# A mixture-of-experts layer at the end of a three-layer program: the order in which the first two pairs of heads choose their experts and fetch the expert rows

## The chip, the cores and the metric

The program runs on one core of one Trainium2 chip. Its time is the device time of one execution in microseconds (us); several executions are timed and their median is given. Everything is computed in float32; weights are split into a high and a low part so that three fast matrix products make one of nearly full precision.

## What is computed

Two blocks of one kind and one of another run after each other on 256 tokens of width 2048. The change touches only the last sublayer, which looks up single-neuron experts ("PEER") for each token:

```python
q = (hb @ w_query).reshape(PEER_BLOCK, PEER_HEADS, 2, D_KEY // 2)
s = jnp.einsum('thpc,hpnc->thpn', q, sub_keys)
top_s, top_i = lax.top_k(s, PEER_TOPK)                      # 16 of 128, twice per head
cand_s = (top_s[:, :, 0, :, None] + top_s[:, :, 1, None, :]).reshape(PEER_BLOCK, PEER_HEADS, -1)
best_s, best_j = lax.top_k(cand_s, PEER_TOPK)               # 16 of 256 per head
idx = jnp.take_along_axis(cand_i, best_j, axis=-1)          # expert numbers
g = jax.nn.softmax(best_s, axis=-1)
a = jax.nn.gelu(jnp.einsum('thkd,td->thk', jnp.take(u, idx, axis=0), hb), approximate=False)
out = jnp.einsum('thk,thkd->td', g * a, jnp.take(v, idx, axis=0))
```

There are 8 heads, 16 experts per head and token, and two blocks of 128 tokens. Each expert is one row of 2048 numbers (8 KB) in the table u and one in the table v, both of 16384 rows in HBM.

## The kernel before

One function, `order()`, yields the whole program as a list of steps, and each engine's function walks that same list and issues its own part of each step. So the order of the yields is the order of every engine's queue. Long pieces of work are generators in a "lane" (X, Y, M); `pump` advances a lane by so many steps, `drain` runs it to its end.

The work of the last sublayer, for which `order()` has the lines below "late_loads":

- **The query projection**, 32 weight pieces (numbered q = 0 to 31 here, four column groups of 8). SyncE loads each piece of 512 KB into one of the 4 slots of `ring`; ScalarE rounds it to the high part `wH` (L603); VectorE subtracts to get the low part `wL` (L1102, "the split"), which also frees the ring slot; TensorE multiplies (24 matmuls of 128x256 a piece, out to `tp`). There are 3 buffers of wH and wL, and the split for piece q + 2 stands ahead of piece q.
- **The choice of experts** (`choose(i)`) for a pair of heads and a block of 128 tokens; there are 8 such pairs, i = 0 to 7. It runs on VectorE: the scores of four lists are reduced to their best 16 (`top16`: max, index, replace, max, index), sums of pairs are formed, the best 16 of 256 taken for each of two heads, and the expert numbers are worked out by comparison with a row of constants (L1628 to L1641) and written to `ix` (L1646). Then come the transposed numbers `ixT` and the softmax weights. In all 10 steps of the lane X.
- **The dot products** (`dot(i, j)`, j = 0 to 31): GpSimd issues an indirect DMA (L2303) that gathers, for column j, one row of u for each of the 128 tokens into a slot (128x2048, 1 MB), and VectorE multiplies it with the tokens and sums (L1729).
- **The v blocks** (`vmix(i, b)`, b = 0 to 7): 4 gathers each from v into slots, and 32 small matmuls (L1770, `pp<-slot,S`) that add weighted rows to the result in `pp`. They need `gelu(i)` on ScalarE and `blend(i)` on VectorE (L1739 to L1746), which need all 32 dots of the pair.

There are 11 slots (`gs`): three in P and SY and two in x (0 to 4), two that lie over the weight ring (5, 6; free once the last split is done) and four in `late` (7 to 10; they lie over the projection's operands and are free once its last matmul is done). `slots()` gives the gathers, in the order of issue, their slots: the first 16 go round slots 0 to 4, after that all 11 go round. A gather into a slot waits until the dot or v block that used it is done.

In the kernel before, choose(0) is advanced 1.25 steps a piece in the pieces 8 to 15, and then drained; dot (0, j) goes with piece 16 + j. The other 16 dots of pair 0 follow the projection, with choose(1) advanced 0.65 steps a dot between them. From pair 1 on, each pair's 32 dots have the 8 v blocks of the pair before among them (one block behind every fourth dot), and choose(i + 1) at 0.42 steps a dot.

## Time and profile before

| | us |
|---|---|
| median of 3 runs | 3189.14 |
| lowest and highest | 3184.85, 3191.65 |
| the profiled execution | 3189.19 |
| its span, first to last instruction | 3187.3 |
| VectorE busy | 1688.7 |
| TensorE busy | 2167.2 |
| GpSimd busy | 790.4 |

The profile counts microseconds from the start of the span. PE is TensorE (PEld its weight loads), DVE VectorE, ACT ScalarE, POOL GpSimd. The last sublayer runs from about 1800 us to the end. In a timeline row the first number is the start, the second the duration, and the brackets at its end hold the idle time before it and what ended it. "DMA share" is the mean busy share of the 16 DMA engines and "GB/s" what they moved. The granted clock of TensorE is 1.00 at 2.4 GHz and 0.50 at 1.2 GHz.

### The profile page before, as it was taken

The numbers are of one execution on the slowest core, as the hardware profiler recorded it, in microseconds if no ns is written. First come the engines' busy times: TensorE is split into PE (matmuls) and PEld (weight loads), VectorE is DVE, ScalarE is ACT, GpSimd is POOL, SyncE is SP. The second block draws the span as 40 slices with busy tenths as digits, with TensorE's granted clock in tenths as the row PEclk, the third lists the DMA queues.
The fourth block names the chain that finished last, engine by engine and source line by source line (L and its number), as shares of the span: only waits on it lengthen the run. The fifth ranks groups of instructions, "written<-read, shape, count | busy, mean of one in ns | idle before, by whom it ended". The sixth has DMA issues, their size and how long they took to land.

```text
span 3187.3 us, 30704 instructions
## 1 busy us (share of the span) xinstructions
PE 2167.2 (68%) x12338; PEld 1485.5 (47%) x12338; DVE 1688.7 (53%) x2571; ACT 852.9 (27%) x1267; POOL 790.4 (25%) x680
## 2 busy tenths in 40 slices
PE   5899999989999999999989970323223232232335
PEld 2666677877788787666668870000000000000001
DVE  3436456554656664343336688656565556565430
ACT  1333443443444454544545420000000000000000
POOL 1111100000000000000000026555555555555552
PEclk8999999999999999999989995666666666656667
DMA  9788865557665555343225687999999999999998
GB/s 387 282 289 270 287 209 155 181 173 236 213 186 151 157 160 176 106 132 120 92 80 186 204 317 315 422 421 421 422 422 422 421 422 422 422 421 422 422 421 342
DMA packets 243593, 901.00 MB, mean 283 GB/s; under 512 B 20374, under 2 KB 45228, under 8 KB 177004
## 3 DMA queue, kind: packets, MB, share of 16 engines
q0 software_dynamic: 94208, 612.85, 47.9%
q1 hardware_dynamic: 148768, 285.58, 27.7%
q8 instruction: 97, 1.59, 0.2%
q10 hardware_dynamic: 476, 0.62, 0.1%
q14 instruction: 44, 0.36, 0.0%
HBM read 894.78 MB, written 2.10 MB: 281 GB/s over the span
## 4 chain that ended last, share of the span: by engine, by line
PE 55%; DMA 31%; DVE 8%; ACT 3%; issue 2%; POOL 1%; another core or an unknown queue 1%; SPq 0%; DVEq 0%; ACTq 0%; POOLq 0%
PE pp L1770 47%; DMA late<-in_peer_v,MI 10%; PE tp L1770 6%; DMA P<-in_peer_v,MI 5%; DMA ring<-in_peer_v,MI 5%; DMA x<-in_peer_v,MI 4%; DMA SY<-in_peer_v,MI 2%; DVE wL L1102 2%; PE tp L1773 2%; DMA late<-in_w_mod 2%; ACT wH L603 1%; DMA ring<-in_peer_w_query 1%; DMA ring<-in_w_in 1%; DMA P<-in_w_mod 0%
## 5 line engine op out<-in xcount | busy, mean ns | idle before, releaser
L1102 DVE TENSOR_TENSOR wL<-ring,wH 128x1024 fp32r<-128x1024 f32 (+3 forms) x504 | 583.7, 1162 | 768.5 <-ACT wH L603 767.2
L1770 PE MATMUL pp<-wH,hH 128*128 128x512 f32 (+3 forms) x1888 | 747.2, 396 | 16.4 <-issue 7.9
L603 ACT ACTIVATE wH<-ring 128x1024 fp32r<-128x1024 f32 (+3 forms) x504 | 507.7, 1010 | 791.3 <-PE pp L1770 646.8
L1770 PE MATMUL pp<-wH,hL 128*128 128x512 f32 (+3 forms) x1888 | 717.7, 380 | 0.0
L1770 PE MATMUL pp<-wL,hH 128*128 128x512 f32 (+3 forms) x1888 | 717.4, 380 | 0.0
L1770 PEld LDWEIGHTS pp<-wH,hH 128*128 128x128 f32 x1888 | 359.7, 191 | 160.5 <-issue 90.7
L1770 PE MATMUL pp<-late,S 128*32 128x512 f32 x736 | 231.6, 893 | 295.4 <-DMA SY<-in_peer_v,MI 75.7
L1770 PEld LDWEIGHTS pp<-wH,hL 128*128 128x128 f32 x1888 | 359.1, 190 | 63.5
L1770 PEld LDWEIGHTS pp<-wL,hH 128*128 128x128 f32 x1888 | 360.3, 191 | 55.9 <-issue 1.0
L1770 PE MATMUL pp<-P,S 128*32 128x512 f32 x376 | 267.0, 877 | 146.7 <-DMA x<-in_peer_v,MI 74.3
L1770 PE MATMUL pp<-x,S 128*32 128x512 f32 x376 | 166.5, 879 | 222.1 <-DMA ring<-in_peer_v,MI 222.1
L1729 DVE CUSTOM_DVE_ANT_0 late<-late,P 128x2048 f32<-128x2048 f32 x88 | 200.6, 2288 | 169.8 <-DMA late<-in_peer_u,MI 169.8
L1770 PE MATMUL pp<-ring,S 128*32 128x512 f32 x376 | 167.3, 889 | 148.4 <-DMA late<-in_peer_v,MI 148.4
L1770 PEld LDWEIGHTS pp<-late,S 128*32 128x32 f32 x736 | 51.8, 156 | 392.8 <-issue 392.8
L2313 POOL DMA_DIRECT2D P<-in_w_mod x85 | 45.0, 529 | 612.2 <-DVE hL L1145 314.5
L1003 ACT ACTIVATE MI<-MI 128x32 f32<-128x32 f32 x8 | 1.8, 229 | 685.2 <-DVE MI L1649 685.2
L1770 PE MATMUL pp<-SY,S 128*32 128x512 f32 x184 | 131.7, 883 | 77.0 <-DMA P<-in_peer_v,MI 77.0
L1729 DVE CUSTOM_DVE_ANT_0 P<-P 128x2048 f32<-128x2048 f32 x50 | 114.4, 2288 | 96.0 <-DMA P<-in_peer_u,MI 96.0
L1770 PEld LDWEIGHTS pp<-x,S 128*32 128x32 f32 x376 | 35.0, 154 | 272.7 <-issue 272.7
L1729 DVE CUSTOM_DVE_ANT_0 x<-x,P 128x2048 f32<-128x2048 f32 x49 | 111.8, 2287 | 89.3 <-DMA x<-in_peer_u,MI 89.3
L2303 POOL DMA_INDIRECT late<-in_peer_u,MI x88 | 146.0, 1659 | 49.4 <-issue 26.5
L2289 POOL DMA_DIRECT2D U<-in_norm_ffn x1 | 0.5, 533 | 610.5 <-PE pp L1770 610.5
(303 smaller groups left out, 2964.2 us busy)
## 6 DMA issues: line engine op xcount, KB each, us to landing
ring<-in_w_in SPq DMA_DIRECT2D x288, 512.0 KB, 3.9
ring<-in_w_out SPq DMA_DIRECT2D x96, 512.0 KB, 4.4
P<-in_w_mod POOLq DMA_DIRECT2D x85, 512.0 KB, 5.0
late<-in_w_mod SPq DMA_DIRECT2D x64, 512.0 KB, 9.1
SY<-in_w_mod POOLq DMA_DIRECT2D x43, 512.0 KB, 5.1
ring<-in_w_in SPq DMA_DIRECT2D x48, 368.0 KB, 4.3
ring<-in_peer_w_query SPq DMA_DIRECT2D x32, 512.0 KB, 5.1
ring<-in_w_in SPq DMA_DIRECT2D x24, 344.0 KB, 3.2
```

What stands on the lines that cost most here:

```text
L603: act(heads(wH[k % NB][:, 0:2 * wd], 2), raw, ACT.Copy).then_inc(*tick("act_hi", ("hi", k)))
L1003: act(c3, c3, ACT.Exp).then_inc(*tick("act_x", ("gap exp", i)))
L1102: tt(lo, raw, hi.bitcast(F32), ALU.subtract).then_inc(*tick("dve_lo", *names))
L1729: e.tensor_tensor_reduce(out=gs[slot], in0=gs[slot], in1=hn[i // 4], scale=1.0, scalar=0.0, op0=ALU.mult, op1=ALU.add, accum_out=aa[i % 2] ...
L1770: return e.matmul(o, l, r, start=start, stop=stop, skip_group_check=skip)
L1773: return e.transpose(o, i, ident[0:k, 0:k])
L2289: e.dma_start(to, src).then_inc(*landed(sem, *names))
L2303: e.indirect_dma_start(gs[slot], None, tab[0], bass.IndirectOffsetOnAxis(ap=picks, axis=0)).then_inc(*landed(f"expert_in{slot}", ("gathere ...
L2313: e.dma_start(mod_in[b], I["w_mod"][l, k * 128:(k + 1) * 128, c0:c0 + 1024]).then_inc(*landed(f"mod_in{b}", ("mod", m)))
```

## The change

Three things change, all in the last sublayer.

1. **choose(0) works head by head.** For i = 0 the generator does everything for the first head (two `top16` of 128, the sums, one `top16` of 256, the expert numbers) and then for the second, 6 steps each, on operands of half the width; then the common tail, a 13th step. The expert numbers of the two heads are announced apart, and the gather for column j waits only for head j // 16. It is advanced 4 steps a piece from piece 8 on, and drained behind piece 11.
2. **Dots from piece 12 on.** Dot (0, j) goes with piece 12 + j, so 20 of the 32 stand beside the projection and 12 behind it. The slots 0 to 4 serve the first 22 gathers instead of the first 16.
3. **choose(1) moves behind all 32 dots of pair 0.** Nothing of it stands between the dots; behind dot (0, 31) come gelu, blend and the first three v blocks of pair 0, and then choose(1) as a whole. The other five v blocks of pair 0 stand among the dots of pair 1, behind every sixth.

```diff
 NB, NS, NG = 3, 4, 11
+FIRST_DOT = 12
@@ order()
         if g == 1:
-            yield from pump(1.25, 0, 0)
-        if g == 1 and pc == 7:
+            yield from pump(4, 0, 0)
+        if q == FIRST_DOT - 1:
             yield "drain", "X"
-        if g >= 2:
-            yield "dot", 0, 8 * g - 16 + pc
+        if q >= FIRST_DOT:
+            yield "dot", 0, q - FIRST_DOT
     for i in range(8):
         if i < 7:
             yield "scores", i + 1
             yield "open", "X", "choose", i + 1
-        for j in range(0 if i else 16, 32):
+        for j in range(0 if i else 32 - FIRST_DOT, 32):
             yield "dot", i, j
...
-            if i and j == 1:
+            if i > 1 and j == 1:
                 yield "blend", i - 1
-            if i and j % 4 == 3:
+            if i > 1 and j % 4 == 3:
                 yield "vmix", i - 1, j // 4
-            yield from pump(0.42 if i else 0.65, 0, 0)
-        yield "drain", "X"
+            if i == 1 and j % 6 == 5:
+                yield "vmix", 0, 3 + j // 6
+            if i:
+                yield from pump(0.42, 0, 0)
+        if i:
+            yield "drain", "X"
         yield "gelu", i
+        if i == 0:
+            yield "blend", 0
+            for b in range(3):
+                yield "vmix", 0, b
+            yield "drain", "X"
@@ slots()
-                if n == 16:
+                if n == 34 - FIRST_DOT:
                     queue = list(range(5, NG)) + queue
@@ choose(i) on VectorE
+                for h0, h1 in ((0, 2),) if i else ((0, 1), (1, 2)):
+                    nh, ps = h1 - h0, slice(16 * h0, 16 * h1)
+                    for b in range(2 * h0, 2 * h1):
+                        top16(sc[i % 2][:, b * 128:(b + 1) * 128], tv[:, b, :], ti[:, b, :])
+                        yield
...
-                copy(ix[i % 4], fa).then_inc(*tick("dve_x", ("experts", i)))
+                    copy(ix[i % 4][:, ps], fa[:, ps]).then_inc(*tick("dve_x", *[("experts", i, h) for h in range(h0, h1)]))
+                    yield
@@ dot on GpSimd
-                    w.wait_ge(*at("experts", i))
+                    w.wait_ge(*at("experts", i, j // 16))
```

On VectorE, in the pieces 13 to 15 of the projection, the program before has these rows (`TENSOR_TENSOR wL<-ring,wH` is a split, the other rows belong to choose(0)):

```order
L1102 TENSOR_TENSOR wL<-ring,wH 128x1024
L1628 TENSOR_SCALAR MI<-MI 128x32
L1632 CAST MI<-MI 128x32
L1636 TENSOR_TENSOR U<-MI,CW 128x256 x2
L1639 TENSOR_TENSOR U<-U,MI 128x512
L1641 TENSOR_REDUCE MI<-U 128x32
L1102 TENSOR_TENSOR wL<-ring,wH 128x1024
L1630 TENSOR_SCALAR MI<-MI 128x32
L1632 CAST MI<-MI 128x32
L1636 TENSOR_TENSOR U<-MI,CW 128x256 x2
L1639 TENSOR_TENSOR U<-U,MI 128x512
```

After the change this stands a few pieces earlier, between the splits of the pieces 11 and 12:

```order
L1112 TENSOR_TENSOR wL<-ring,wH 128x1024
L1641 TENSOR_SCALAR MI<-MI 128x16
L1645 CAST MI<-MI 128x16
L1649 TENSOR_TENSOR U<-MI,CW 128x256
L1652 TENSOR_TENSOR U<-U,MI 128x256
L1655 TENSOR_REDUCE MI<-U 128x16
L1643 TENSOR_SCALAR MI<-MI 128x16
L1645 CAST MI<-MI 128x16
L1649 TENSOR_TENSOR U<-MI,CW 128x256
L1652 TENSOR_TENSOR U<-U,MI 128x256
L1655 TENSOR_REDUCE MI<-U 128x16
L1659 SCALAR_TENSOR_TENSOR MI<-MI 128x16
```

One step stood between two splits; now four do, and the expert numbers of one head (16 columns) are made between two splits, without the other head's.

On GpSimd, from the first gather into the weight ring's slots (the 17th of all) on, before:

```order
L2303 DMA ring<-in_peer_u,MI 128x2048 x2
L2303 DMA late<-in_peer_u,MI 128x2048 x4
L2303 DMA P<-in_peer_u,MI 128x2048
L2303 DMA SY<-in_peer_u,MI 128x2048
L2303 DMA x<-in_peer_u,MI 128x2048 x2
L2303 DMA P<-in_peer_u,MI 128x2048
L2303 DMA ring<-in_peer_u,MI 128x2048 x2
L2303 DMA late<-in_peer_u,MI 128x2048 x4
L2303 DMA P<-in_peer_u,MI 128x2048
L2303 DMA SY<-in_peer_u,MI 128x2048
L2303 DMA x<-in_peer_u,MI 128x2048
L2303 DMA x<-in_peer_v,MI 128x2048
```

And from the same place on after the change (now the 23rd gather):

```order
L2319 DMA ring<-in_peer_u,MI 128x2048 x2
L2319 DMA late<-in_peer_u,MI 128x2048 x4
L2319 DMA SY<-in_peer_u,MI 128x2048
L2319 DMA x<-in_peer_u,MI 128x2048 x2
L2319 DMA P<-in_peer_u,MI 128x2048
L2319 DMA P<-in_peer_v,MI 128x2048
L2319 DMA ring<-in_peer_v,MI 128x2048 x2
L2319 DMA late<-in_peer_v,MI 128x2048 x4
L2319 DMA SY<-in_peer_v,MI 128x2048
L2319 DMA x<-in_peer_v,MI 128x2048 x2
L2319 DMA P<-in_peer_v,MI 128x2048 x2
L2319 DMA ring<-in_peer_u,MI 128x2048 x2
```

Before, 16 gathers for the rest of pair 0 and 4 for pair 1 stood ahead of the first gather from v; now the last 10 of pair 0 stand there, and 12 gathers from v ahead of the first of pair 1.

On VectorE, near the end of pair 0's dots (`ISA slot,MI<-slot,P` is a dot), before:

```order
L1729 ISA ring,MI<-ring,P 128x2048
L1729 ISA MI 128x1
L1630 TENSOR_SCALAR MI<-MI 128x32
L1632 CAST MI<-MI 128x32
L1636 TENSOR_TENSOR U<-MI,CW 128x256 x2
L1639 TENSOR_TENSOR U<-U,MI 128x512
L1641 TENSOR_REDUCE MI<-U 128x32
L1729 ISA late,MI<-late,P 128x2048
L1729 ISA MI 128x1
L1729 ISA late,MI<-late,P 128x2048
L1729 ISA MI 128x1
```

At the end of pair 0's dots after the change:

```order
L1745 ISA P,MI<-P 128x2048
L1745 ISA MI 128x1
L1755 TENSOR_TENSOR MI<-MI 128x32
L1757 STREAM_TRANSPOSE MI<-MI 128x32
L1762 TENSOR_TENSOR S<-MI 128x1024
L1604 MAX MI<-U 128x8
L1606 MAX_INDEX MI<-MI,U 128x8
L1608 MATCH_REPLACE U<-MI,U 128x128
L1610 MAX MI<-U 128x8
L1612 MAX_INDEX MI<-MI,U 128x8
```

The steps of choose(1) lay between the dots of pair 0. Now the dots run without them, the blend (the rows of L1755 to L1762) follows the last dot, and choose(1) begins behind it.

## Rows read from the trace of the kernel before

**Rows 1.** The page: span, and DMA busy tenths and GB/s in 40 slices.

```profile
span 3187.3 us, 30704 instructions
...
DMA  9788865557665555343225687999999999999998
GB/s 387 282 289 270 287 209 155 181 173 236 213 186 151 157 160 176 106 132 120 92 80 186 204 317 315 422 421 421 422 422 422 421 422 422 422 421 422 422 421 342
```

**Rows 2.** Stretches: us, busy PE, PEld, DVE, ACT, POOL (count), PEclk, DMA share, GB/s.

```profile
1820.00:1860.00 40.00, 34.44 (x271) 33.86 (x269) 31.34 (x82) 15.12 (x16) 5.11 (x5) 0.96 0.58 188
1860.00:1908.00 48.00, 37.68 (x268) 35.68 (x269) 39.39 (x37) 11.53 (x11) 15.72 (x11) 0.93 1.02 405
1908.00:1916.00 8.00, 7.56 (x62) 7.17 (x60) 8.00 (x8) 1.60 (x2) 4.65 (x2) 1.00 0.32 96
1916.00:1956.00 40.00, 0.21 (x2) 0.02 (x1) 38.30 (x75) 0.00 (x0) 26.35 (x14) 0.54 1.00 408
1956.00:1972.00 16.00, 0.00 (x0) 0.00 (x0) 15.51 (x29) 1.51 (x2) 2.20 (x2) 0.50 0.07 16
1972.00:1980.00 8.00, 0.00 (x0) 0.00 (x0) 4.85 (x5) 2.09 (x3) 6.78 (x5) 0.50 0.99 381
1980.00:3100.00 1120.00, 327.37 (x1824) 86.23 (x1828) 623.69 (x894) 20.53 (x29) 619.33 (x450) 0.63 1.01 422
```

**Rows 3.** Timeline of POOL: gathers from u.

```profile
1851.23 1.01 POOL L2303 DMA_INDIRECT P<-in_peer_u,MI  x1 [51.51 <-DVE MI L1655]
...
1860.56 1.68 POOL L2303 DMA_INDIRECT P<-in_peer_u,MI  x1 [2.99 <-DVE MI L1729]
...
1903.18 1.68 POOL L2303 DMA_INDIRECT P<-in_peer_u,MI  x1 [2.89 <-DVE MI L1729]
1911.02 2.75 POOL L2303 DMA_INDIRECT ring<-in_peer_u,MI  x1 [6.15 <-DVE wL L1102]
...
1944.68 1.91 POOL L2303 DMA_INDIRECT late<-in_peer_u,MI  x1 [0.30 <-issue]
1969.50 0.94 POOL L2303 DMA_INDIRECT late<-in_peer_u,MI  x1 [22.91 <-DVE MI L1649]
```

**Rows 4.** Timeline of DVE in the query projection: splits, first choice, dots.

```profile
1821.86 1.23 DVE L1102 TENSOR_TENSOR wL<-ring,wH 128x1024 fp32r<-128x1024 f32 x1 [0.70 <-ACT wH L603]
1824.35 0.29 DVE L1594 MAX8 MI<-U 128x8 f32<-128x128 f32 x1 [1.26 <-ACT U L1058]
...
1848.82 1.22 DVE L1102 TENSOR_TENSOR wL<-ring,wH 128x1024 fp32r<-128x1024 f32 x1
...
1857.99 2.29 DVE L1729 CUSTOM_DVE_ANT_0 P<-P 128x2048 f32<-128x2048 f32 x1 [4.97 <-DMA P<-in_peer_u,MI]
...
1865.50 2.28 DVE L1729 CUSTOM_DVE_ANT_0 SY<-SY,P 128x2048 f32<-128x2048 f32 x1
...
1868.85 2.28 DVE L1729 CUSTOM_DVE_ANT_0 x<-x,P 128x2048 f32<-128x2048 f32 x1
...
1881.16 2.29 DVE L1729 CUSTOM_DVE_ANT_0 P<-P 128x2048 f32<-128x2048 f32 x1
...
1887.19 2.29 DVE L1729 CUSTOM_DVE_ANT_0 SY<-SY,P 128x2048 f32<-128x2048 f32 x1
```

**Rows 5.** Timeline of DVE: the last split, the last dot of pair 0, blend(0).

```profile
1909.53 1.22 DVE L1102 TENSOR_TENSOR wL<-ring,wH 128x1024 fp32r<-128x1024 f32 x1
...
1970.24 2.29 DVE L1729 CUSTOM_DVE_ANT_0 late<-late,P 128x2048 f32<-128x2048 f32 x1
...
1980.67 1.22 DVE L1746 TENSOR_TENSOR S<-MI 128x1024 f32<-128x1024 f32 x1
```

**Rows 6.** Stretches of 4 us, columns as in rows 2.

```profile
1840.00:1844.00 4.00, 2.24 (x19) 2.04 (x18) 3.79 (x12) 1.06 (x1) 0.00 (x0) 1.00 0.17 53
1844.00:1848.00 4.00, 4.00 (x23) 4.00 (x22) 3.86 (x8) 0.99 (x1) 0.00 (x0) 0.57 0.44 135
1848.00:1852.00 4.00, 4.00 (x35) 3.92 (x34) 3.41 (x12) 1.46 (x4) 0.77 (x1) 1.00 0.52 157
```

More of the change, by code:

```diff
@@ L998, in choose @@
             def choose(i):
-                for _ in range(9):
+                for _ in range(9 if i else 12):
                     yield
@@ L1610, in choose @@
                     w.wait_ge(*at("mixed", i - 3, 7))
-                for b in range(4):
-                    top16(sc[i % 2][:, b * 128:(b + 1) * 128], tv[:, b, :], ti[:, b, :])
-                    yield
-                chain()
-                copy(tf, ti).then_inc(*tick("dve_x"))
+                io = CW[:, INV + 64:INV + 80]
                 t0 = tv.rearrange("p (h s) k -> p h s k", s=2)
                 f0 = tf.rearrange("p (h s) k -> p h s k", s=2)
-                tt(ca.rearrange("p (h a b) -> p h a b", h=2, a=16), t0[:, :, 0, :].unsqueeze(3).to_broadcast([128, 2, 16, 16]),
-                   t0[:, :, 1, :].unsqueeze(2).to_broadcast([128, 2, 16, 16]), ALU.add).then_inc(*tick("dve_x"))
@@ L1620, in choose @@
-                yield
-                for h in range(2):
-                    top16(ca[:, h * 256:(h + 1) * 256], bv[:, h, :], heads(bj, 2)[:, h, :])
-                    yield
-                io = CW[:, INV + 64:INV + 80]
-                for s in range(2):
+                c0 = ca.rearrange("p (h a b) -> p h a b", h=2, a=16)
+                for h0, h1 in ((0, 2),) if i else ((0, 1), (1, 2)):
[3 more added lines that the diff above has]
+                        yield
+                    chain()
+                    copy(tf[:, 2 * h0:2 * h1, :], ti[:, 2 * h0:2 * h1, :]).then_inc(*tick("dve_x"))
+                    tt(c0[:, h0:h1], t0[:, h0:h1, 0, :].unsqueeze(3).to_broadcast([128, nh, 16, 16]),
+                       t0[:, h0:h1, 1, :].unsqueeze(2).to_broadcast([128, nh, 16, 16]), ALU.add).then_inc(*tick("dve_x"))
+                    yield
+                    for h in range(h0, h1):
+                        top16(ca[:, h * 256:(h + 1) * 256], bv[:, h, :], heads(bj, 2)[:, h, :])
+                        yield
+                    for s in range(2):
+                        chain()
+                        if s == 0:
+                            e.tensor_scalar(bh[:, ps], bj[:, ps], 4, None, ALU.logical_shift_right).then_inc(*tick("dve_x"))
+                        else:
+                            e.tensor_scalar(bh[:, ps], bj[:, ps], 15, None, ALU.bitwise_and).then_inc(*tick("dve_x"))
+                        chain()
+                        copy(fa[:, ps], bh[:, ps]).then_inc(*tick("dve_x"))
+                        chain()
+                        for h in range(h0, h1):
+                            fh = fa[:, h * 16:(h + 1) * 16].unsqueeze(2).to_broadcast([128, 16, 16])
+                            tt(oh[:, h, :, :], fh, io.unsqueeze(1).to_broadcast([128, 16, 16]), ALU.is_equal).then_inc(
+                                *tick("dve_x"))
+                        chain()
+                        tt(oh[:, h0:h1], oh[:, h0:h1], f0[:, h0:h1, s, :].unsqueeze(2).to_broadcast([128, nh, 16, 16]),
+                           ALU.mult).then_inc(*tick("dve_x"))
+                        chain()
+                        e.tensor_reduce(heads(fi[s], 2)[:, h0:h1], oh[:, h0:h1], AX, ALU.add).then_inc(*tick("dve_x"))
+                        if s == 0:
+                            yield
@@ L1626, in choose @@
                     chain()
-                    if s == 0:
-                        e.tensor_scalar(bh, bj, 4, None, ALU.logical_shift_right).then_inc(*tick("dve_x"))
-                    else:
-                        e.tensor_scalar(bh, bj, 15, None, ALU.bitwise_and).then_inc(*tick("dve_x"))
+                    stt(fa[:, ps], fi[0][:, ps], 128.0, fi[1][:, ps], ALU.mult, ALU.add).then_inc(*tick("dve_x"))
                     chain()
-                    copy(fa, bh).then_inc(*tick("dve_x"))
@@ L1633, in choose @@
-                    chain()
-                    for h in range(2):
-                        fh = fa[:, h * 16:(h + 1) * 16].unsqueeze(2).to_broadcast([128, 16, 16])
-                        tt(oh[:, h, :, :], fh, io.unsqueeze(1).to_broadcast([128, 16, 16]), ALU.is_equal).then_inc(
-                            *tick("dve_x"))
-                    chain()
-                    tt(oh, oh, f0[:, :, s, :].unsqueeze(2).to_broadcast([128, 2, 16, 16]), ALU.mult).then_inc(*tick("dve_x"))
-                    chain()
@@ L2194, in choose @@
             def choose(i):
-                for _ in range(10):
+                for _ in range(10 if i else 13):
                     yield
```

4 lines of the change are left out of this document (removed).

## The prediction

> **What bounds the kernel now.** I read the page's slices first. From slice 26 on, about 2000 us, the DMA engines are full and move 421 or 422 GB/s to the end, but for the last slice [rows 1]; the stretches confirm it, 1120 us at a share of 1.01 and 422 GB/s, with 450 gathers issued, one in 2.49 us [rows 2]. A gather is 128 rows of 8 KB, 1.049 MB, and 1.049 MB at 422 GB/s is also 2.49 us; a weight piece, half as much, is 1.24 us. In that time VectorE is busy 624 of 1120 us and TensorE 327 [rows 2]. So from 1980 us on the end of the kernel is set by the bytes that are left, and no engine's work there counts. The number of bytes doesn't change. What the change can win or lose is the time in which the DMA engines stand idle before they are full for good. So the sum is one of idle DMA time from 1820 us on.
>
> Before, against 422 GB/s [rows 2]: 1820 to 1860, 40 x (1 - 188/422) = 22.2 us; 1860 to 1908, 1.9; 1908 to 1916, 6.2; 1916 to 1956, 1.3; 1956 to 1972, 15.4; 1972 to 1980, 0.8. Together **47.8 us**. Three holes make it up. The first lies ahead of the first gather, which goes out at 1851.23 when choose(0) is done. The second, at 1908, is the 17th gather waiting 6.15 us for the last split (it goes into the ring) while the one ahead of it had gone at 1903.18. The third is choose(1): GpSimd issues the last gather of pair 0 at 1944.68 and then stands 22.91 us until 1969.50, when the expert numbers of pair 1 are there [rows 3]. VectorE, between 1916 and 1972, is busy 54 of 56 us [rows 2], since it does 16 dots and the whole of choose(1) there.
>
> **The change, part by part.**
>
> *The first choice.* Its first step starts at 1824.35 and the gathers go at 1851.2: 26.9 us with seven splits of 1.22 us among them, the last at 1848.82 [rows 3, 4], so choose(0) by itself takes about 19 us. Head by head it issues more and shorter instructions: the expert-number part runs twice on half the width. If nothing but the fixed cost of the small ones grows, that is 1 us, if halving saved nothing, some 4; I take 2. The scores don't come earlier. The first head's numbers need half of the 19 us less the common tail, some 9 to 10 us, and one split: the first gather goes at **about 1835.5** instead of 1851.2. Slots 3 and 4 need nothing later than what was there. The whole choice and four splits (4.9 us) take 19 + 2 + 4.9 = 26 us, and the first dot starts at about 1850.3, at once, since its rows are there; before it started at 1857.99 after 4.97 us of waiting [rows 4].
>
> *DMA until the first dot.* From 1820 to 1835.5 the DMA engines have only weights. A load goes out for each split, and there are three (1819.9, 1821.86 and about 1831): 3.7 us of work, **11.8 us idle**. From 1835.5 to the first release at 1852.5 there are five gathers and three loads, 12.5 + 3.7 = 16.2 of 17 us; a gather takes some time to start (5 us passed from the first issue to a DMA that kept pace), so I take **3 us** idle (1 to 6).
>
> *Pieces 12 to 31.* VectorE does a split and a dot a piece, 3.35 us (1865.50 to 1868.85 [rows 4]). The last split is 17 pieces behind the first dot: 1850.3 + 57 = 1907, against 1909.53 before [rows 5]. What the DMA engines must move from 1852.5 until then: the 17 gathers that dots 0 to 16 release, 42.3 us, and 13 loads, 16.1 us, 58.4 us in all for 55 us. They are full but for accidents; before they lost 1.9 us in 48 us [rows 2]. I take **4 us** idle (2 to 11), since slots 0 to 4 alone serve this stretch and TensorE starts it with a low clock (below). The 6.2 us hole goes: gathers 21 and 22 (the 17th to 22nd now use slots 0 to 4) wait for dots only, and the 23rd, into the ring, stands behind the last split in any case. SyncE's queue has only the loads and isn't passed by anything.
>
> *Behind the projection.* The remaining gathers of pair 0 come at 2.49 us each against 2.2 us a dot, so VectorE keeps up. GpSimd issued 16 there back to back, at 2.2 us each (1911.02 to 1944.68 is 33.7 us for 15 intervals [rows 3]), just under 2.49; the loss was 1.3 us in 40, and I take **1 us** (0 to 3). Counting bytes, gathers 6 to 32 and the loads (27 x 2.49 + 16.1 = 83.3 us, and 5 us idle) end at about 1941, so dot (0, 31) ends at T = 1943.5, where it started at 1970.24 before [rows 5].
>
> *The hand-over to pair 1.* GpSimd has 12 gathers from v queued at once behind pair 0's; they need a released slot each and the numbers, which have long been there. Eleven of the twelve wait only for dots up to (0, 31); the twelfth waits for the first v block on TensorE. They are 29.9 us of DMA work from T - 2.5, until T + 27.4. Against that: gelu and blend on VectorE, about 2 us (its largest part is 1.22 us [rows 5]), then choose(1) without anything between, 19 us less its tail of 1.3: the numbers of pair 1 at T + 20, seven microseconds before the DMA engines run dry. Cost **0**, and what hides choose(1) are the twelve gathers; if that cover is short, each microsecond beyond T + 27 is lost. The range takes 0 to 8. Behind VectorE's drain of choose(1) no dot is waiting, since no row of pair 1 has been asked for. ScalarE's exponent for choose(1) now stands behind gelu(0); it follows the numbers and holds up only the tail. What is late next is the bytes.
>
> Sum of idle time after: 11.8 + 3 + 4 + 1 + 0 = 19.8 us, bounded by 15 and 39. With 2 us for what I can't see in a trace of before, 22. The gain is 47.8 - 22 = 26 us, and the profiled execution's 3189.19 us, which lies at the median of 3189.14, becomes **3163 us**.
>
> TensorE's clock bears on one term. From 1840 to 1844 TensorE was busy 2.24 of 4 us, and in the next 4 us its clock was granted at 0.57, nearly all at 1.2 GHz, with 23 matmuls instead of 35; then it was back at 1.00 [rows 6]. Four steps between two splits, 6 to 7.5 us, leave TensorE idle longer than that three times over, so it will start the pieces with dots at the low level. A full-speed piece is 24 of those matmuls, 2.7 us, a slow one 5.5 us, above the 3.35 us of VectorE. One or two slow pieces cost at most 4 us, inside the range above. The Trainium skill, "TensorE: Matmul & The Clock Gate", Part 1, states a rule that speaks against such gaps: idle time takes the clock to half, and sustained work brings it back. By that rule the row's recovery would repeat here, and the sum would stay; only work too broken up to bring it back would make the second rival.
>
> **The rivals.** *A, the hand-over is not covered, or the front gains less* (the v gathers wait for slots, choose(1) takes longer than 20 us, the dots' stretch loses 10 us): 8 to 18 us of the gain go, 3171 to 3181. For it speaks that the margin is 7 us and rests on eleven slots being free in time; against it that each part has a row.
>
> *B, TensorE stays at 1.2 GHz through the pieces with dots.* Then a piece takes 5.5 us and the last split comes at 1850.3 + 17 x 5.5 = 1944. DMA has 58.4 us of work in 91.5, 33 us idle instead of 4: 51 us in all, 3192 at most, no difference that counts. Against it: in the dots' stretch before, from 1860 to 1908, the clock was 0.93 in the mean [rows 2].
>
> *C, slower.* The pieces with dots go at 6.0 us each, as 1881.16 to 1887.19 [rows 4], because weight loads queue behind five outstanding gathers, and yet the DMA engines aren't full, as each gather waits for its dot and each dot for its split. 17 x 6.0 = 102 us for 58.4 us of work is 44 us idle, 62 with the rest: 14 us slower, 3203. It decides from 5.8 us a piece on. Against it: where pieces went at 6 us before, DMA was full (405 GB/s over the stretch [rows 2]), so what was late were bytes that had to move anyway.
>
> *D, the order is changed but the holes stay as they are*: the program's own order shows the gathers from v ahead of pair 1's, so this needs both holes to be made by something else than the waits named: 3186 to 3192.
>
> **How the numbers follow.** A difference within 0.2% (6.4 us) is about what a measurement of this kernel can't tell from none. The forecast, 3154 to 3170: 0.70. A: 0.17, all of it still faster by over 0.2%. B and D: 0.08, the same. C and other ways to be slower: 0.05. The range takes in the forecast's case and most of A, with the spread of the runs (3 us to either side): 3154 to 3176. Faster 0.87, same 0.08, slower 0.05.
>
> **What would show it.** The first gather at 1835 to 1837; the first dot by 1852, with no wait for DMA; the last split at 1905 to 1915; no gather held up by it; the first gather from v before 1935; GpSimd not standing over 10 us for the numbers of pair 1; from 1855 on no 20 us under 380 GB/s. Wrong would be a stretch between 1940 and 1990 below 300 GB/s, a clock of 0.5 from 1855 to 1905, or pieces over 4 us apart with idle DMA engines.

## The result: 0.85% faster, and the profile after

| | before | after |
|---|---|---|
| median, us | 3190.39 | 3162.44 |
| lowest and highest of 4 runs | 3184.85, 3191.94 | 3158.22, 3164.52 |
| ratio of the medians, 95% interval | | 0.9915 (0.9903 to 0.9926) |
| span of the profiled execution | 3187.3 | 3159.6 |
| busy: TensorE, VectorE, GpSimd | 2167.2, 1688.7, 790.4 | 2164.9, 1692.1, 806.4 |

The forecast was 3163 us, 26 less than before; measured are 3162.44 in the median. VectorE has 3.4 us more to do (the halves of choose(0)). GpSimd has 16 more, 12.6 of them between 1980 and 3100 us, where the mean issue of a gather takes 1.41 us instead of 1.38. TensorE's busy time differs by 2.3 us. No engine lost work worth naming, and the program is 28 us shorter; the same kernel timed again was 24 us shorter than the kernel before beside it (the second table below). The page of the kernel after, span and DMA in 40 slices, to be held against [rows 1]:

```profile
span 3159.6 us, 30717 instructions
...
DMA  9888865557665555343325689999999999999998
GB/s 385 285 294 271 287 213 153 181 166 243 207 190 157 152 178 158 116 134 106 107 86 162 207 323 406 422 422 421 422 421 422 421 422 420 422 421 422 421 422 338
```

Slice 24 stood at 315 GB/s (there it is 1912 to 1992 us) and stands at 406 (now 1896 to 1975). Slice 23, 1833 to 1912 before and 1817 to 1896 after, went only from 317 to 323: it now begins 16 us earlier, ahead of the choice, and so takes in the whole hole in front of the first gather. Everything behind is full as before. The stretches of the kernel after answer to [rows 2] (us, busy PE, PEld, DVE, ACT, POOL with counts, PEclk, DMA share, GB/s):

```profile
1820.00:1836.00 16.00, 10.76 (x89) 10.36 (x87) 13.51 (x48) 3.88 (x5) 0.77 (x1) 1.00 0.31 102
1836.00:1852.00 16.00, 9.59 (x46) 9.39 (x47) 14.72 (x41) 2.12 (x3) 4.00 (x5) 0.62 0.94 354
1852.00:1916.00 64.00, 56.17 (x427) 53.88 (x427) 57.61 (x54) 18.73 (x18) 28.14 (x18) 0.95 1.02 401
1916.00:1928.00 12.00, 3.12 (x18) 2.93 (x17) 12.00 (x11) 2.97 (x3) 10.17 (x7) 0.64 0.91 328
1928.00:1980.00 52.00, 14.47 (x88) 4.02 (x92) 40.78 (x92) 1.74 (x3) 32.37 (x23) 0.63 1.01 423
1980.00:3100.00 1120.00, 326.10 (x1837) 86.24 (x1832) 624.70 (x893) 21.21 (x30) 631.91 (x448) 0.64 1.01 421
```

Against 422 GB/s, 12.1 us are idle up to 1836, 2.6 up to 1852, 3.2 up to 1916, 2.7 up to 1928, and none between 1928 and 1980, where before there were 15.4 and 0.8. GpSimd's timeline has the steps behind that, as [rows 3] before (start, duration, and in brackets the idle time and what ended it):

```profile
1835.23 1.01 POOL L2319 DMA_INDIRECT P<-in_peer_u,MI  x1 [36.79 <-DVE MI L1606]
...
1852.36 1.67 POOL L2319 DMA_INDIRECT P<-in_peer_u,MI  x1 [11.15 <-DVE MI L1745]
...
1911.09 0.93 POOL L2319 DMA_INDIRECT P<-in_peer_u,MI  x1 [1.67 <-DVE MI L1745]
1913.80 2.74 POOL L2319 DMA_INDIRECT ring<-in_peer_u,MI  x1 [1.78 <-DVE wL L1112]
...
1936.83 2.17 POOL L2319 DMA_INDIRECT P<-in_peer_v,MI  x1 [0.30 <-issue]
...
1961.39 0.93 POOL L2319 DMA_INDIRECT P<-in_peer_v,MI  x1 [4.24 <-PE pp L1786]
1969.28 0.94 POOL L2319 DMA_INDIRECT ring<-in_peer_u,MI  x1 [6.96 <-DVE MI L1665]
```

The first gather goes at 1835.23, the first from v at 1936.83. GpSimd stands 1.78 us for the last split where it stood 6.15, and 6.96 us for the numbers of pair 1 where it stood 22.91. VectorE's timeline, as [rows 4, 5]:

```profile
1822.65 0.29 DVE L1604 MAX8 MI<-U 128x8 f32<-128x128 f32 x1 [1.26 <-ACT U L1068]
...
1849.80 2.29 DVE L1745 CUSTOM_DVE_ANT_0 P<-P 128x2048 f32<-128x2048 f32 x1
...
1853.15 2.28 DVE L1745 CUSTOM_DVE_ANT_0 P<-P 128x2048 f32<-128x2048 f32 x1
...
1877.93 1.22 DVE L1112 TENSOR_TENSOR wL<-ring,wH 128x1024 fp32r<-128x1024 f32 x1 [2.21 <-ACT wH L613]
...
1912.31 1.23 DVE L1112 TENSOR_TENSOR wL<-ring,wH 128x1024 fp32r<-128x1024 f32 x1 [1.49 <-ACT wH L613]
...
1945.84 2.29 DVE L1745 CUSTOM_DVE_ANT_0 P<-P 128x2048 f32<-128x2048 f32 x1 [0.19 <-DMA P<-in_peer_u,MI]
...
1948.90 1.22 DVE L1762 TENSOR_TENSOR S<-MI 128x1024 f32<-128x1024 f32 x1
```

The first row is the first step of choose(0); the first dot starts at 1849.80 with no wait in brackets; the second, 3.35 us later, has a split ahead of it. Then a split that waited 2.21 us for ScalarE's `wH` (the weight load behind it was late), the last split, the last dot of pair 0, and the large row of blend(0).

**A measure for the experiments.** The stretch ahead of the first choice is the same code in all kernels here, and yet its length differs between profiled executions: the choice started at 1814.2 to 1826.0 us. That noise is in every median. So beside the median I use two numbers of each profile that it doesn't touch. **Rest** is the end of the span less the start of the first step of choose(0). **Idle** is the sum, over stretches of 4 us from 4 us ahead of that start and for about 190 us, of 4 x (1 - GB/s / 422). If the end is set by bytes, rest less idle must be the same in all kernels. It was 1314.9 to 1317.1 us in all twelve profiles (eleven kernels, one of them twice). So each difference in rest between two kernels is, within 2 us, a difference in idle DMA time, and the view of stretches says where it lies. Two profiles of the kernel after differ by 2.0 us in rest, which is what this measure can tell. Of the 27.7 us by which the span fell, 26.1 are rest and 1.7 are the start of the choice, which came that much earlier; that part is the noise just named. Below, "above after" means above the mean rest of these two profiles, 1337.9 us.

| kernel | median, us | ratio to before (95%) | rest | idle |
|---|---|---|---|---|
| before | 3190.39 | | 1363.0 | 47.9 |
| after | 3162.44 | 0.9915 (0.9903, 0.9926) | 1336.9 | 21.3 |
| after_again | 3163.91 | 0.9929 (0.9915, 0.9942) | 1338.9 | 21.8 |
| handover_alone | 3176.28 | 0.9956 (0.9942, 0.9970) | 1350.0 | 33.2 |
| front_alone | 3185.9 | 0.9987 (0.9977, 0.9996) | 1361.6 | 45.4 |
| slots_at_18 | 3173.56 | 0.9945 (0.9929, 0.9961) | 1345.6 | 28.7 |
| dots_from_16 | 3170.49 | 0.9936 (0.9920, 0.9953) | 1343.8 | 28.6 |
| two_v_blocks | 3168.23 | 0.9941 (0.9925, 0.9958) | 1344.2 | 29.3 |
| whole_choice | 3169.79 | 0.9947 (0.9931, 0.9964) | 1347.0 | 31.1 |
| choice_plus_8 | 3165.55 | 0.9928 (0.9913, 0.9944) | 1341.9 | 24.8 |
| choice_plus_28 | 3179.39 | 0.9976 (0.9968, 0.9985) | 1355.9 | 39.8 |
| six_steps | 3163.66 | 0.9925 (0.9911, 0.9938) | 1341.4 | 24.4 |

The kernels were run in four groups, each beside its own runs of the kernel before (medians 3190.39, 3188.74, 3186.9, 3187.96), so a ratio belongs to its group. One of the six runs of dots_from_16 was slow, at 3928.3 us; the ratios use fast runs alone.

### The profile page after: what moved, and what is told of

Same layout as the page of the kernel before. It is cut to its first block, busy times and chain, and to the rows that moved or that the text cites. A ratio compares the mean times of both kernels' runs of the same rounds, so it can differ in the third digit from the quotient of the medians.

```text
span 3159.6 us, 30717 instructions
## 1 busy us (share of the span) xinstructions
PE 2164.9 (69%) x12338; PEld 1487.2 (47%) x12338; DVE 1692.1 (54%) x2583; ACT 853.3 (27%) x1267; POOL 806.4 (26%) x680
## 4 chain that ended last, share of the span: by engine, by line
PE 56%; DMA 30%; DVE 7%; ACT 3%; issue 2%; POOL 2%; SPq 0%; DVEq 0%; ACTq 0%; POOLq 0%
PE pp L1786 48%; DMA late<-in_peer_v,MI 9%; PE tp L1786 6%; DMA P<-in_peer_v,MI 5%; DMA x<-in_peer_v,MI 5%; DMA ring<-in_peer_v,MI 4%; DMA SY<-in_peer_v,MI 2%; DVE wL L1112 2%; PE tp L1789 2%; DMA late<-in_w_mod 2%; ACT wH L613 1%; DMA ring<-in_peer_w_query 1%; POOL late L2319 1%; DMA ring<-in_w_in 1%; DMA P<-in_w_mod 0%
## 5 line engine op out<-in xcount | busy, mean ns | idle before, releaser
L1786 PE MATMUL pp<-wH,hH 128*128 128x512 f32 (+3 forms) x1888 | 747.8, 396 | 16.2 <-issue 7.9
L1745 DVE CUSTOM_DVE_ANT_0 late<-late,P 128x2048 f32<-128x2048 f32 x84 | 191.3, 2288 | 154.0 <-DMA late<-in_peer_u,MI 153.8
L1786 PE MATMUL pp<-P,S 128*32 128x512 f32 x360 | 157.8, 873 | 166.8 <-DMA late<-in_peer_v,MI 91.4
L1786 PE MATMUL pp<-ring,S 128*32 128x512 f32 x344 | 153.0, 868 | 139.9 <-DMA late<-in_peer_v,MI 139.9
L1786 PE MATMUL pp<-SY,S 128*32 128x512 f32 x200 | 141.6, 874 | 90.4 <-DMA P<-in_peer_v,MI 90.4
L1745 DVE CUSTOM_DVE_ANT_0 P<-P 128x2048 f32<-128x2048 f32 x53 | 120.9, 2287 | 91.4 <-DMA P<-in_peer_u,MI 91.4
L2319 POOL DMA_INDIRECT late<-in_peer_v,MI x96 | 115.1, 1199 | 172.2 <-PE pp L1786 148.1
L1745 DVE CUSTOM_DVE_ANT_0 ring<-ring,P 128x2048 f32<-128x2048 f32 x47 | 107.2, 2288 | 75.3 <-DMA ring<-in_peer_u,MI 75.3
```

The source lines that it names most:

```text
L1745: e.tensor_tensor_reduce(out=gs[slot], in0=gs[slot], in1=hn[i // 4], scale=1.0, scalar=0.0, op0=ALU.mult, op1=ALU.add, accum_out=aa[i % 2] ...
L1786: return e.matmul(o, l, r, start=start, stop=stop, skip_group_check=skip)
L2319: e.indirect_dma_start(gs[slot], None, tab[0], bass.IndirectOffsetOnAxis(ap=picks, axis=0)).then_inc(*landed(f"expert_in{slot}", ("gathere ...
```

## The experiments

The theory: the time is the bytes and the idle time of the DMA engines; each part of the change takes idle time out of one of three holes. The rivals: one part does it all; the part's gain comes from less waiting on the engines and not from the DMA engines; or a part gains nothing because the hole it fills opens elsewhere.

### The hand-over alone

```diff
@@ kernel before, order()
-            if i and j == 1:
+            if i > 1 and j == 1:
                 yield "blend", i - 1
-            if i and j % 4 == 3:
+            if i > 1 and j % 4 == 3:
                 yield "vmix", i - 1, j // 4
-            yield from pump(0.42 if i else 0.65, 0, 0)
-        yield "drain", "X"
+            if i == 1 and j % 6 == 5:
+                yield "vmix", 0, 3 + j // 6
+            if i:
+                yield from pump(0.42, 0, 0)
+        if i:
+            yield "drain", "X"
         yield "gelu", i
+        if i == 0:
+            yield "blend", 0
+            for b in range(3):
+                yield "vmix", 0, b
+            yield "drain", "X"
```

> The kernel before with the third part of the change alone: choose(1) behind all 32 dots of pair 0 and behind blend and three v blocks, the first choice and the dots of the projection as before. Theory (idle DMA time sets the time, and twelve queued gathers from v cover choose(1)): the hole of 15.4 us at 1956 and the 0.8 us behind it go, the other holes stay, so 15 to 16 us faster than before, about 3174. Rival (choose(1) is on the path wherever it stands): within 5 us of before, 3185 to 3195, with GpSimd again standing some 20 us for the numbers of pair 1.

Measured: 3176.28 us, rest 13.0 us below before, where I had expected 15 to 16. Two stretches of this kernel:

```profile
1908.00:1916.00 8.00, 7.21 (x57) 6.77 (x56) 8.00 (x9) 1.22 (x2) 3.87 (x2) 1.00 0.31 104
1956.00:1980.00 24.00, 6.34 (x33) 1.65 (x34) 21.95 (x68) 1.51 (x2) 14.00 (x11) 0.57 1.01 420
```

And two gathers of its GpSimd timeline:

```profile
1911.82 2.74 POOL L2312 DMA_INDIRECT ring<-in_peer_u,MI  x1 [6.16 <-DVE wL L1111]
...
1982.67 0.94 POOL L2312 DMA_INDIRECT P<-in_peer_u,MI  x1 [5.85 <-DVE MI L1658]
```

The hole at 1908 is as before, 104 GB/s, with GpSimd waiting 6.16 us for the last split. The hand-over's hole is gone: 420 GB/s from 1956 to 1980, though GpSimd stood 5.85 us for the numbers of pair 1. So the cover by the gathers from v is real and worth 13 us by itself. Idle time fell by 14.7 us: the 16.2 of the hole went, and 1.3 came back in small parts ahead of 1956 us.

### The front alone

```diff
@@ kernel after, order()
-            if i == 1 and j % 6 == 5:
-                yield "vmix", 0, 3 + j // 6
-            if i:
-                yield from pump(0.42, 0, 0)
-        if i:
-            yield "drain", "X"
+            yield from pump(0.42 if i else 0.87, 0, 0)
+        yield "drain", "X"
         yield "gelu", i
-        if i == 0:
-            yield "blend", 0
-            for b in range(3):
-                yield "vmix", 0, b
-            yield "drain", "X"
```

(and the two conditions `i > 1` back to `i`; so choose(1) stands among the dots of pair 0 again).

> The changed kernel with the third part undone: the first choice head by head, dots from piece 12 and 22 gathers in slots 0 to 4 stay; choose(1) stands between the 12 dots behind the projection, at 0.87 steps a dot, and the v blocks of pair 0 stand behind every fourth dot of pair 1 again. Theory: the first two holes shrink by 7 and 6 us, but pair 0's rows are all in sooner than choose(1) is ready, since VectorE has 15 dots and 19 us of choosing left behind the last split, until about 1959, against 1941 for the DMA engines; the hole at the hand-over grows to 18 us or more, and of 13 us won in front about 10 are left: about 3180. Rival (the parts add up, 26 less the 16 of the hand-over): 13 us or more faster, 3177 or less, with a hole at the hand-over of 15 us as before.

Measured: 3185.9 us, rest only 1.4 us below before and idle time 2.5 us. I had expected some 10. Its stretches and GpSimd's wait:

```profile
1908.00:1916.00 8.00, 5.36 (x43) 4.95 (x41) 5.52 (x6) 2.12 (x2) 2.93 (x2) 1.00 1.00 401
1944.00:1968.00 24.00, 0.00 (x0) 0.00 (x0) 23.20 (x47) 1.51 (x2) 4.48 (x2) 0.50 0.15 53
```

```profile
1963.22 2.74 POOL L2310 DMA_INDIRECT P<-in_peer_u,MI  x1 [25.43 <-DVE MI L1652]
```

The front works: 401 GB/s at 1908 to 1916, no hole. But then the DMA engines run at 53 GB/s from 1944 to 1968, and GpSimd stands 25.43 us. From 1820 us to that hole the idle time is 21.7 us, where before it was 31.6 up to the hole at 1956: 10 us were gained in front. The hole itself has 21.0 us instead of the 16.2 at 1956 to 1980, and the 16 us behind it run at 350 GB/s, which is 2.7 us more. So 7.5 of the 10 were given back at the hand-over. The last gather of pair 0 was issued 110.9 us behind the start of the choice instead of 120.3, 9.4 us sooner. The numbers of pair 1 came only 6.4 us sooner (138.7 instead of 145.2), since choose(1) needs VectorE's time, and the first gather that used them took 2.74 us to issue instead of 0.94, which made the start of the stream another 1.5 us longer (last section). Alone the parts bring 13.0 and 1.4, together 24 to 26 us. **The parts don't add up: what the front gains counts only where the hole behind it is covered.**

### The switch to all slots

```diff
@@ kernel after, slots()
-                if n == 34 - FIRST_DOT:
+                if n == 18:
```

> The changed kernel with slots 0 to 4 serving only the first 18 gathers instead of 22, so that the 19th (and, behind it in GpSimd's queue, all later ones) waits for the last split. Theory: the last gather ahead of that wait goes at about 1894, five gathers in flight last 12.5 us, and DMA stands idle from about 1907 to 1914: 5 to 8 us slower than the changed kernel, 3167 to 3170. Rival (the projection's end is bound by the splits, not by gathers): no difference from the changed kernel, 3160 to 3164.

Measured: 3173.56 us, rest 7.7 us above the mean of the two profiles of after (1337.9), idle 7 us more. I had expected 5 to 8 us, and 3167 to 3170 for the median: the rest fits, the median lies 3.6 us above.

```profile
1900.00:1908.00 8.00, 7.58 (x61) 7.17 (x60) 8.00 (x9) 1.07 (x1) 1.68 (x1) 1.00 1.02 410
1908.00:1916.00 8.00, 7.36 (x57) 6.75 (x57) 8.00 (x8) 2.13 (x2) 0.43 (x1) 1.00 0.20 81
```

```profile
1915.57 2.75 POOL L2319 DMA_INDIRECT ring<-in_peer_u,MI  x1 [12.85 <-DVE wL L1112]
```

81 GB/s at 1908 to 1916: the 19th gather stands 12.85 us for the last split, and everything behind it in GpSimd's queue stands too. This line of the change, which looks like bookkeeping, is worth about 8 us. (The switch can't be put as far forward as the 17th gather: that gather is what dot 16 reads, it would wait for the last split, and that split stands behind dot 16 on VectorE. This wasn't tried.)

### Dots from piece 16

```diff
-FIRST_DOT = 12
+FIRST_DOT = 16
```

> The changed kernel with the dots of pair 0 from piece 16 on as before (16 beside the projection, 16 behind it; slots 0 to 4 serve 18 gathers), the first choice still head by head at four steps a piece, drained now behind piece 15, the hand-over as changed. Theory: five gathers are in at about 1850 and no slot is released before the first dot at about 1862, so DMA idles some 6 to 10 us more there; the rest is as in the changed kernel: 3168 to 3173. Rival (the early first gathers do nothing, and only the hand-over counts): as the hand-over alone, 3174 to 3176.

Measured: 3170.49 us, rest 5.9 us above after. The first gather goes at the same offset, but then:

```profile
1848.00:1868.00 20.00, 20.00 (x161) 20.00 (x160) 12.67 (x12) 7.94 (x8) 3.36 (x2) 0.95 0.73 251
```

```profile
1832.19 1.01 POOL L2319 DMA_INDIRECT P<-in_peer_u,MI  x1 [36.78 <-DVE MI L1606]
...
1861.49 1.68 POOL L2319 DMA_INDIRECT P<-in_peer_u,MI  x1 [23.30 <-DVE MI L1745]
```

Five gathers fill five slots, and GpSimd stands 23.30 us until the first dot has freed one; the DMA engines have little but weights meanwhile, 251 GB/s in 20 us. So early gathers need early dots.

### Two v blocks ahead of the choice

```diff
@@ kernel after, order()
-            if i == 1 and j % 6 == 5:
-                yield "vmix", 0, 3 + j // 6
+            if i == 1 and j % 5 == 4:
+                yield "vmix", 0, 2 + j // 5
...
-            for b in range(3):
+            for b in range(2):
                 yield "vmix", 0, b
```

> The changed kernel with two v blocks ahead of choose(1) instead of three (the other six behind every fifth dot of pair 1). Theory: eight gathers from v are 19.9 us of DMA work, over 17.4 us behind the last dot of pair 0, and the numbers of pair 1 come 21 us behind it, so DMA idles 4 to 8 us: 3166 to 3171. Rival (the third block isn't needed; DMA has other work or the gap is found again later): 3160 to 3164.

Measured: 3168.23 us, rest 6.3 us above after.

```profile
1952.00:1964.00 12.00, 6.28 (x40) 1.63 (x36) 9.20 (x30) 0.23 (x1) 2.30 (x3) 0.75 0.46 170
```

```profile
1961.09 0.94 POOL L2319 DMA_INDIRECT x<-in_peer_u,MI  x1 [15.86 <-DVE MI L1665]
```

With four gathers fewer (10 us of transfers) the engines run dry before the numbers are there: 170 GB/s in 12 us, 7.2 us idle. GpSimd stands 15.86 us instead of 6.96.

### The choice as a whole, between the same splits

```diff
@@ kernel after, choose(i) on VectorE
-                for h0, h1 in ((0, 2),) if i else ((0, 1), (1, 2)):
+                for h0, h1 in ((0, 2),):
```

(with the number of steps in the other engines' lists set to match).

> The changed kernel with the first choice not head by head: both heads at once in 10 steps as before, but still four steps a piece and dots from piece 12. Theory: the first gather goes when the whole choice is done, at about 1845 instead of 1835; the dots can't start before the first row is in, at about 1851, so little is lost on VectorE, and DMA idles some 6 us more at the front: 3166 to 3170. Rival (only the dots' start counts, and the rows were there early anyway): no difference, 3160 to 3164.

Measured: 3169.79 us, rest 9.1 us above after. First the gather that starts it all, then the stretches:

```profile
1845.92 1.01 POOL L2319 DMA_INDIRECT P<-in_peer_u,MI  x1 [45.76 <-DVE MI L1671]
```

```profile
1820.00:1836.00 16.00, 12.47 (x93) 12.27 (x92) 13.17 (x46) 4.24 (x5) 0.00 (x0) 0.85 0.38 124
1836.00:1848.00 12.00, 7.81 (x35) 7.22 (x35) 10.99 (x31) 2.44 (x4) 1.77 (x2) 0.64 0.20 54
```

The first gather goes 21.9 us behind the start of the choice, 9.3 us later than in after (12.6), and the DMA engines are idle 9.8 us more. Some 8 of these lie in front, with the 54 GB/s from 1836 to 1848, and most of the rest behind the projection. I had expected some 6. Nothing later made up for any of it.

### More work in choose(1)

```diff
@@ kernel after, choose(i) on VectorE
+                if i == 1:
+                    for _ in range(8):      # 28 in the second kernel
+                        chain()
+                        tt(U[:, 1536:2048], U[:, 1536:2048], U[:, 1536:2048], ALU.max).then_inc(*tick("dve_x"))
```

The added steps leave an unused part of U as it is. They stand ahead of choose(1), behind blend(0).

> The changed kernel with 8 extra VectorE instructions of 128x512 ahead of choose(1), some 6 us (they work on a buffer that isn't in use and change nothing). Theory: the numbers of pair 1 had 6.7 us to spare before the last gather of v block 2 landed, so 0 to 4 us of the 6 show (a gather takes some microseconds to get going): 3162 to 3166. Rival (choose(1) is on the path): all 6 show, 3168.

> The changed kernel with 28 such extra instructions ahead of choose(1), some 20 us. Theory: the cover is used up and what goes beyond it shows in full: 20 less the 3 to 7 us to spare, 13 to 17 us slower than the changed kernel, 3175 to 3179, with one hole of that length in the DMA row about 1976. Rival (choose(1) is on the path): 20 us slower, 3182; rival (the later dots catch up): under 10 us slower.

Measured with 8: 3165.55 us, rest 4.0 above after. VectorE's added group (its second number is the time it takes), and GpSimd's first gather of pair 1:

```profile
1950.59 5.77 DVE L1624 TENSOR_TENSOR U<-U 128x512 f32<-128x512 f32 x8
```

```profile
1975.63 0.95 POOL L2323 DMA_INDIRECT ring<-in_peer_u,MI  x1 [11.46 <-DVE MI L1669]
```

With 28: 3179.39 us, rest 18.0 above after, for these 20.30 us:

```profile
1948.29 20.30 DVE L1624 TENSOR_TENSOR U<-U 128x512 f32<-128x512 f32 x28
```

```profile
1987.85 0.95 POOL L2323 DMA_INDIRECT ring<-in_peer_u,MI  x1 [25.71 <-DVE MI L1669]
```

```profile
1970.00:1974.00 4.00, 1.20 (x12) 0.16 (x4) 3.62 (x19) 0.00 (x0) 0.00 (x0) 0.93 0.75 311
1974.00:1988.00 14.00, 7.61 (x40) 2.54 (x40) 12.98 (x44) 0.20 (x2) 0.15 (x1) 0.74 0.00 0
1988.00:1992.00 4.00, 0.00 (x0) 0.00 (x0) 0.55 (x3) 0.61 (x2) 3.09 (x4) 0.50 0.64 193
```

With 8 steps the result is at the upper end of what I had expected (0 to 4 us), with 28 it is 1 us over (13 to 17). If seven microseconds had been free, 8 steps (5.8 us) would have cost nothing and 28 some 13 to 14. By the rest, 1.8 of 5.8 us and 2.3 of 20.3 were free.

The last view says where the others went. The engines run dry at about 1973.0 (311 GB/s is 3 of the 4 us to 1974), which is 152.5 us behind the start of the choice. The gather with the new numbers is issued at 1987.85, and its start costs idle time too: the 0.15 us up to 1988 and, at 193 GB/s, 2.2 of the next 4 us, 2.3 in all. The hole is thus 1987.85 + 2.3 - 1973.0 = 17.2 us, for 20.3 us of added work: 3.1 were free. With 8 steps the hole between 1974 and 1979 is 3.2 us for 5.8, so 2.6 were free. In the kernel after the numbers are there at 1969.28 and would need the same 2.3 us, 1971.6; the dry point would be 1975.1 by the 152.5 us of this kernel, and 1974.0 by the one with 8 steps (151.4). All readings lie between 2 and 3.5 us of slack, which is as far as they can be told apart. The start of a gather on idle engines counts as work of the hand-over.

### The kernel after once more, and one with six steps

```diff
-FIRST_DOT = 12
+FIRST_DOT = 11
@@ order()
-            yield from pump(4, 0, 0)
+            yield from pump(6, 0, 0)
```

> The changed kernel as it is, once more, for comparison on the same chip with the next one. From the start of the first choice to the end of the span it took 1336.9 us; both theories expect 1336 to 1338 again, and a median of 3160 to 3166.

> The changed kernel with six steps of the first choice a piece instead of four, so that one head's choice lies between two splits, and dots from piece 11 (21 beside the projection, slots 0 to 4 for 23 gathers). Theory (time is idle DMA time): the first gather goes one split, 1.1 us, earlier, and as much of the hole in front of it goes; the splits that come later cost nothing: 1 to 2 us less from the start of the first choice to the end, 1335 to 1336, which the medians hardly tell apart. Rival (TensorE, which now waits longer and starts the pieces with dots later and at the low clock, becomes the bound): 2 us or more slower, 1339 or more.

Measured: 3163.91 us for the same kernel again, its rest 1338.9 us, 0.9 above what I had expected. For six steps 3163.66 us beside it, and a rest of 1341.4, where I had expected 1335 to 1336. The first gather does go 1.0 us sooner, 11.6 us behind the start of the choice instead of 12.6, but a stretch about the last split more than takes that back:

```profile
1908.00:1920.00 12.00, 7.81 (x51) 7.40 (x50) 7.69 (x7) 2.12 (x2) 4.19 (x3) 0.86 0.76 297
```

297 GB/s over 12 us is 3.6 us idle. Between 85 and 112 us behind the start of the choice, where the last split lies, this kernel has 5.7 us of idle time, and the two profiles of after have 2.8 and 4.1; ahead of that, from 29 us on, it has 3.7 against 2.9 and 2.1. GpSimd stands 4.96 us for a dot and 2.83 us for the last split, and the last two splits stand 2.5 us each for ScalarE's `wH`, which stands 4.9 us for its weight load. The rest of 1341.4 lies in the range that I had given to the rival, TensorE as the bound. But TensorE's clock is 0.97 in the mean from 1856 to 1908 us, and the waits named are for weights, so these rows don't show the rival's cause; what put the weights late wasn't tested. Rest is 2.5 to 4.5 us above after, the medians are the same. The version isn't better, and by the medians the choice of four steps isn't a sharp optimum.

## Why the prediction was right, point by point

**The measure of the sum.** The forecast was made in idle time of the DMA engines: 47.8 us before, 22 after, a gain of 26. The profiles have 47.9 and 21.3, and rest fell by 26.1 (24.1 in the second profile). That rest less idle stays within 2.2 us over eleven kernels is what shows the form of the sum to be right, and not only its result. (The upper bounds of its terms add up to 39.8 us, not 39.) That the result came out to a microsecond is partly luck: the terms below were off by +0.3, -0.4, -0.8 and +1.7 us, and 2 us had been added for what couldn't be seen. The median moved by 28 us in one group of runs and by 24 in the other.

**The front.** The first gather was put at 1835.5, 11.2 us behind the start of the choice; it went at 1835.23, but the choice itself had started 1.7 us earlier in this profile, so the offset is 12.6: 1.4 us over. The first head's steps end at 1834.35, which is 10.6 us without the one split (put at 9 to 10), and the gather goes 0.9 us behind them. Idle until then was put at 11.8, measured 12.1 up to 1836. The start of the first gathers and the stretch to the first release was put at 3, measured 2.6. The first dot was put 26 us behind the start and went 27.2 behind it, at once as forecast.

**Pieces 12 to 31.** The last split was put 82.7 us behind the start and came 89.7 behind it: seven microseconds over. Splits stood three times, 2.2, 2.6 and 1.5 us, for weight loads, while the DMA engines moved 401 GB/s; the rest is mainly the later first dot. The first pieces of the stretch went at 3.35 us each. It cost nothing, for the reason that I gave against rival C: what was late were bytes that had to move anyway. The idle time, put at 4, was 3.2. The 23rd gather was held up by the split, 1.78 us; the sum has it behind the last split, and yet the list of signs says that no gather is held up by it.

**Behind the projection.** Put at 1 us, measured 2.7, in 1916 to 1928 at 328 GB/s. Of this, 1.2 us lie in 1916 to 1918 (164 GB/s), right behind the 23rd gather, which first waited for the split and then took 2.74 us to issue. In the 6 us behind that the engines move some 340 GB/s. The slots of the ring and `late` are free by then: GpSimd has no wait but its own issuing, one gather in 2.21 us, and is busy 10.17 of 12 us with 7 instructions. So the late 23rd gather and GpSimd's pace are what the rows offer as causes; no run separates them. The second profile of after has 1.3 us more about here than the first, so this term isn't the same from one execution to the next. So the sentence that from 1855 on no 20 us would be below 380 GB/s was wrong: from 1912 to 1932 they move 364. This term was mis-sized by under 2 us.

**Dot (0, 31)** was to end 119 us behind the start and ended at 1948.13, 125.5 behind it. I had counted too few bytes behind the first release: 83.3 us of work, while the queues moved 29.3 MB of gathers and 7.7 MB of weights from 1852.5 to 1946, which is 88 us at 422 GB/s and 15 weight pieces instead of 13. So the first gather from v went at 1936.83, where the signs had it before 1935. It shifted where things lie, and not the end.

**The hand-over.** Put at 0 with seven microseconds of margin; it was 0, with 2 to 3.5. The step that was mis-sized is the margin: the numbers came 21.15 us behind the last dot (put at 20), the engines would have run dry 26 to 27 us behind it (27.4), and what I left out is the start of the stream, 2.3 us of idle time. I had used that very cost in the front, where I allowed 3 us, and not here. Rival A's threshold was thus nearer than the text said; the two experiments with added work show it, and with two v blocks, which leave 10 us less cover, the hole opens.

**TensorE's clock.** Forecast: one or two slow pieces, then full speed. The kernel after in stretches of 4 us, as [rows 6]:

```profile
1844.00:1848.00 4.00, 0.81 (x4) 0.73 (x4) 3.65 (x13) 0.55 (x2) 0.00 (x0) 0.82 1.00 390
1848.00:1852.00 4.00, 4.00 (x21) 4.00 (x20) 3.63 (x4) 1.57 (x2) 0.00 (x0) 0.50 1.03 419
1852.00:1856.00 4.00, 4.00 (x30) 4.00 (x30) 4.00 (x6) 1.07 (x1) 1.96 (x2) 0.83 1.00 365
1856.00:1860.00 4.00, 4.00 (x36) 4.00 (x35) 4.00 (x5) 2.20 (x3) 2.33 (x2) 1.00 1.00 386
```

TensorE is busy 0.81 of 4 us, then its clock is granted at 0.50 (1.2 GHz) for the next 4 us, at 0.83 in the 4 behind it, and at 1.00 from 1856 on. Over 1852 to 1916 it is 0.95 in the mean, so rival B fell. The Trainium skill, "TensorE: Matmul & The Clock Gate", Part 1, has it that gaps halve the clock and sustained work restores it; the trace agrees. VectorE and the DMA engines had work meanwhile, 365 to 419 GB/s, so the slow piece wasn't on the path.

**The rivals.** D (the holes stay) fell by the stretches. C needed pieces of 6 us and idle DMA engines: two dots did come 5.6 and 6.0 us behind the one ahead, but the DMA engines moved 411 GB/s from 1872 to 1888 meanwhile. Its threshold is also off: with C's own terms, 5.8 us a piece is 58 us of idle time, 10 more than before, and the 6.4 us that decide are reached at about 5.6. A was half seen: no microsecond of it came in after, but its margin was at most half of what was forecast.

What the prediction doesn't say is that the parts don't add up. Its sum took the holes one by one, and for the whole change that is right, since the last one is covered. The expectation for the front alone had seen it in part: of 13 us won, 10 were to be left. Of 10 us won by idle time 2.5 were left, and 1.4 by the rest.

## What to carry to other kernels

Where the end is set by bytes, count the idle time of the DMA engines, hole by hole, and look for each hole's one wait: an edit is worth what it takes out of a hole, and engine work beside a full stream costs nothing. Before moving slow work off the front, cover the hole behind it with transfers that are already in the queue, and count into what they must cover the time that the next transfer needs to get going. Here a gain ahead of an uncovered hole was mostly given back there.
